# First halves of K of six tiles of head 0 computed between the opening modulation blocks, into idle PSUM banks

## What is computed

```python
def hybrid_layer(x, ctx, c, c_ctx, ...):
    mod_lat = jax.nn.silu(c) @ w_ada + b_ada
    mod_ctx = jax.nn.silu(c_ctx) @ w_ada + b_ada
    ...
    p = (rmsnorm(x, norm_w) * (1.0 + sc) + sh) @ w_in
    pc = (rmsnorm(ctx, norm_w) * (1.0 + sc_c) + sh_c) @ w_in
    ...
    x = x + gt * (jnp.concatenate([y_a, y_b], axis=-1) @ w_out)
```

## Time and profile before

| | |
|---|---|
| median of three runs | 2515.84 us (2508.7 to 2517.73) |
| profiled execution | 2515.01 us |
| its span in the profile | 2513.2 us |
| TensorE busy | 2322.5 us, 92% of the span |
| VectorE, ScalarE, GpSimd busy | 1392.0 (55%), 922.2 (37%), 147.3 us (6%) |
| DMA | 328.93 MB, 131 GB/s in the mean |
| mean granted TensorE clock | 0.973 |

### The profile page before, as it was taken

The page is one execution under the profiler, slowest core; times in us unless marked ns, Lnnn a source line. Parts: engine busy times, 40 slices in busy tenths (PEclk is TensorE's granted clock), DMA queues, the critical chain, the costliest instruction groups (busy, mean ns, idle before and its releaser), DMA issues. The chain is left out here.

```text
span 2513.2 us, 38542 instructions
## 1 busy us (share of the span) xinstructions
PE 2322.5 (92%) x13846; PEld 1893.7 (75%) x13846; DVE 1392.0 (55%) x2345; ACT 922.2 (37%) x1695; POOL 147.3 (6%) x187
## 2 busy tenths in 40 slices
PE   6799999999999999999999879999999999999797
PEld 3168787878778787878788658788787878878696
DVE  0334646555564646555654455657656575665654
ACT  3432424242423324242522364342424334242423
POOL 0000000000000000000100300000001000000002
PEclk8899999999999999999999979999999999999898
DMA  8973435242433434352535524343424333342453
GB/s 320 352 221 107 142 95 151 84 141 85 125 109 108 129 100 146 88 151 80 158 117 169 175 85 134 99 121 83 127 78 123 101 102 111 89 130 75 138 163 119
DMA packets 488018, 328.93 MB, mean 131 GB/s; under 512 B 48658, under 2 KB 452278, under 8 KB 487174
## 3 DMA queue, kind: packets, MB, share of 16 engines
q1 hardware_dynamic: 393174, 218.59, 31.0%
q10 hardware_dynamic: 94704, 109.13, 13.3%
q0 software_dynamic: 64, 0.20, 0.0%
HBM read 304.73 MB, written 23.13 MB: 130 GB/s over the span
## 5 line engine op out<-in xcount | busy, mean ns | idle before, releaser
L1712 PE MATMUL ps<-h_hi,w_hi 128*128 128x512 f32 (+1 forms) x2080 | 824.3, 396 | 19.1 <-DVE w_lo L1072 10.9
L1714 PE MATMUL ps<-h_hi,w_lo 128*128 128x512 f32 (+1 forms) x2080 | 765.9, 368 | 0.0
L1713 PE MATMUL ps<-h_lo,w_hi 128*128 128x512 f32 (+1 forms) x2080 | 764.2, 367 | 0.0
L1072 DVE TENSOR_TENSOR w_lo<-w_raw,w_hi 128x1024 fp32r<-128x1024 f32 (+1 forms) x332 | 399.5, 1204 | 319.0 <-ACT w_hi L616 269.8
L616 ACT CAST w_hi<-w_raw 128x1024 fp32r<-128x1024 f32 (+1 forms) x332 | 342.0, 1030 | 421.2 <-PE ps L1714 174.9
L1712 PEld LDWEIGHTS ps<-h_hi,w_hi 128*128 128x128 f32 x2080 | 399.1, 192 | 123.0 <-issue 52.4
L1714 PEld LDWEIGHTS ps<-h_hi,w_lo 128*128 128x128 f32 x2080 | 396.8, 191 | 67.6
L1713 PEld LDWEIGHTS ps<-h_lo,w_hi 128*128 128x128 f32 x2080 | 399.9, 192 | 47.7
L1072 DVE TENSOR_TENSOR arena<-arena,ps 128x512 f32<-128x512 f32 (+1 forms) x192 | 117.7, 641 | 109.2 <-PE ps L1803 107.8
L1974 PE MATMUL ps<-h_hi,w_hi 128*128 128x512 f32 (+1 forms) x448 | 160.0, 357 | 13.4 <-DVE h_lo L1072 13.1
L1572 POOL TENSOR_SCALAR small<-small 128x4 f32<-128x4 f32 (+3 forms) x51 | 20.6, 404 | 2300.3 <-DVE small L1425 1017.8
(11 more groups left out here) (191 smaller groups left out, 2692.4 us busy)
## 6 DMA issues: line engine op xcount, KB each, us to landing
w_raw<-in_w_in SPq DMA_DIRECT2D x260, 512.0 KB, 4.0
ada_raw<-in_w_ada ACTq DMA_DIRECT2D x128, 512.0 KB, 4.4
w_raw<-in_w_out SPq DMA_DIRECT2D x64, 448.0 KB, 3.8
arena<-in_w_ada SPq DMA_DIRECT2D x27, 512.0 KB, 8.3
w_raw<-in_w_ada SPq DMA_DIRECT2D x19, 512.0 KB, 8.4
ada_raw<-in_w_ada SPq DMA_DIRECT2D x18, 512.0 KB, 8.3
arena<-decay_rows ACTq DMA_DIRECT2D x16, 512.0 KB, 5.4
x_channel_major<-arena ACTq DMA_DIRECT2D x1, 4096.0 KB, 17.3
```

Source lines behind the costliest of these rows:

```text
L1072: return V.tensor_tensor(o, a, b, op)
L1712: mm(o, w_hi[:, s, k], h_hi[:, kt, t0:], start=kt == 0, stop=False)
L1713: before_last = mm(o, w_hi[:, s, k], h_lo[:, kt, t0:], start=False, stop=False)
L1714: last = mm(o, w_lo[:, s, k], h_hi[:, kt, t0:], start=False, stop=kt == KT - 1)
```

## The change

Six first halves (the small tile and tiles 0 to 4 of head 0; `FIRST[0:6]`) are loaded, split and multiplied in groups 4 to 7 of the opening, three pieces for every two blocks, each tile into a bank of its own (PJ, PJ + 1, G0 to G3). Their second halves follow in the old places. Units are numbered in the new order: 0 to 5 the first halves, 6 to 11 the second halves, then both halves of tiles 5, 6, 7. `w_raw` is out of the ring, which has five buffers now; eight loads of units stand between the blocks in SP's order (`W_AT`), the later ones behind a wait for `w_split`. The splits follow the modulation in each group (`EARLY_SPLITS`). In head 0 the multiplies of w_ada use banks A0 and A1, behind a wait for `rows_copied`.

```diff
-RING = RAW + 5
+EARLY = 6
+RING = 5
...
-        ada_ring = [w_raw[:, s] for s in range(RAW)] + [ada_raw[:, s] for s in range(2)] + [spare[:, s] for s in range(3)]
+        ada_ring = [ada_raw[:, s] for s in range(2)] + [spare[:, s] for s in range(3)]
...
+        FIRST = [(t, half) for half in range(2) for t in range(-1, EARLY - 1)] + [
+            (t, half) for t in range(EARLY - 1, TILES) for half in range(2)]
+        W_AT = {16: 0, 18: 1, 30: 2, 38: 3, 46: 4, 48: 5, 54: 6, 62: 7}
+        EARLY_SPLITS = {2: (0,), 3: (1,), 4: (2, 3), 5: (4,), 6: (5,), 7: (6, 7)}
+        FIRST_SPLITS = {5: 10, 13: 11, 21: 12, 29: 13, 37: 14}
...
 # SP, opening
             for u in range(2 * ADA_START):
...
+                if u in W_AT:
+                    first_unit(W_AT[u])
                 if u >= RING:
                     sp.wait_ge(ada_used, u - RING + 1)
...
 # w_unit
-                if isinstance(i, int) and i * UNITS + u < RAW:
-                    sp.wait_ge(ada_used, last_use[s] + 1)
-                else:
+                if not (isinstance(i, int) and i * UNITS + u < RAW):
                     sp.wait_ge(w_split, i * UNITS + (u - RAW + 1))
...
 # ACT (and DVE with split_lo)
-                if g == 7:
-                    split_hi(0, 0)
                 q = modulated_after(g)
                 if q >= 0:
                     modulate(0, range(4 * q, 4 * q + 4))
+                for u in EARLY_SPLITS.get(g, ()):
+                    split_hi(0, u)
...
 # PE
+            def early_piece(n):
+                u, k = n // HALF, n % HALF
+                if k == 0:
+                    pe.wait_ge(w_split, u + 1)
+                pe.wait_ge(h_ready, k + 1)
+                last = unit_piece(u, tile_bank(0, 0, FIRST[u][0]), 0, 0, [k])
+                if k == HALF - 1:
+                    last.then_inc(w_used, 1)
             for g in range(ADA_START // 4):
                 for pair in range(8):
                     u = 8 * g + pair
+                    for n in range(3 * (u - 32) // 2, 3 * (u - 31) // 2) if u >= 32 else ():
+                        early_piece(n)
                     pe.wait_ge(ada_loaded[u % RING], 16 * (u // RING + 1))
...
                     def ada(k):
...
+                        if is_first(layer, i):
+                            pe.wait_ge(rows_copied, 1)
...
+                            early = is_early(layer, i, t)
+                            u = EARLY + 1 + t if early else base + 2 + k
...
+                            if not (early and half == 0):
+                                last = unit_piece(u, tile_bank(layer, i, t), tokens(layer, t), half,
+                                                  [2 * (s % 4), 2 * (s % 4) + 1])
```

More of the change, by code:

```diff
@@ L507, in load_x, with w_unit, first_unit @@
                 sp.dma_start(x_in[:, n % 2], toks[n // 2][(n % 2) * P:(n % 2 + 1) * P, :]).then_inc(x_loaded[n % 2], 16)
+            def w_unit(i, u, source, tiles=HALF):
+                s = u % RAW
+                if not (isinstance(i, int) and i * UNITS + u < RAW):
+                    sp.wait_ge(w_split, i * UNITS + (u - RAW + 1))
+                    sp.sem_inc(sp_step, 1)
+                dst = w_raw[:, s, 0:tiles]
+                if source.shape[-1] == T:
+                    dst = dst.rearrange("p k n -> p (k n)").rearrange("p (k n) -> p k n", n=T)
+                sp.dma_start(dst, source).then_inc(w_loaded[s], 16)
+            def first_unit(u):
+                t, half = FIRST[u]
+                col = COLUMN[t] if t >= 0 else N_IN - P
+                w_unit(0, u, w_in[0].rearrange("(k p) n -> p k n", p=P)[:, half * HALF:(half + 1) * HALF, col:col + P])
             load_x(0)
@@ L540, in _ @@
                 w_cols = w_in[layer].rearrange("(k p) n -> p k n", p=P)
-                for half in range(2):
+                for half in range(2 if layer else 0):
                     w_unit(0, base + half, w_cols[:, half * HALF:(half + 1) * HALF, N_IN - P:N_IN])
@@ L591, in body @@
                         output_part()
+                        return
+                    if is_first(layer, i):
+                        for u in range(len(W_AT), 2 + UNITS):
+                            first_unit(u)
                         return
@@ L1167, in _ @@
                     modulate(0, range(4 * q, 4 * q + 4))
+                for u in EARLY_SPLITS.get(g, ()):
+                    split_lo(0, u)
             for layer in range(DEPTH):
@@ L1178, in _ @@
                 else:
-                    for u in range(1, LEAD + 1):
-                        split_lo(0, base + u)
+                    for u in range(len(W_AT), len(W_AT) + 2):
+                        split_lo(0, u)
                 vec.wait_ge(x_stored, 16 * (1 + layer * KT))
@@ L1647, in ada_multiply @@
                 for hf in range(2):
-                    pe.wait_ge(ada_loaded[RAW + hf], loads[hf])
+                    pe.wait_ge(ada_loaded[hf], loads[hf])
                     for j in range(HALF // 2):
@@ L1676, in rms, with unit_piece @@
                 spread_rms(n, c0, A1)
+            def unit_piece(u, bank_, t0, half, ks, both=False):
+                s = u % SPLIT
+                for k in ks:
+                    kt = half * HALF + k
+                    o = ps[:, bank_, t0:]
+                    mm(o, w_hi[:, s, k], h_hi[:, kt, t0:], start=kt == 0, stop=False)
+                    before_last = mm(o, w_hi[:, s, k], h_lo[:, kt, t0:], start=False, stop=False)
+                    last = mm(o, w_lo[:, s, k], h_hi[:, kt, t0:], start=False, stop=kt == KT - 1)
+                return (before_last, last) if both else last
+            def early_piece(n):
[6 more added lines that the diff above has]
+                    last.then_inc(w_used, 1)
             for g in range(ADA_START // 4):
@@ L1704, in _ @@
                     rms(layer, 0)
[L1706 to L1711, removed]
-                        mm(o, w_hi[:, s, k], h_hi[:, kt, t0:], start=kt == 0, stop=False)
-                        before_last = mm(o, w_hi[:, s, k], h_lo[:, kt, t0:], start=False, stop=False)
-                        last = mm(o, w_lo[:, s, k], h_hi[:, kt, t0:], start=False, stop=kt == KT - 1)
-                    return (before_last, last) if both else last
                 if layer == 1:
```

76 lines of the change are left out of this document (42 added, 34 removed).

## The result

The changed kernel takes 2551.12 us (median of four, 2547.27 to 2554.30), the kernel before 2516.78 beside it: a ratio of 1.0138, interval 1.0106 to 1.0170. A later set of runs gave 2553.29 against 2513.53, 1.0156 (1.0122 to 1.0190). It is slower by 34 to 40 us, 1.4 to 1.6%. The forecast was 2546 in a range of 2522 to 2558. One slow execution, the profiled one of the version with late splits (2666.45 us at a granted clock of 0.83), is left out of all numbers that follow.

What follows compares the result with a forecast made beforehand. TensorE was taken to bound the run, except the opening, paced by loads. Terms +5.4 + 10.0 + 37.9 - 22.4 = +30.9 us on the profiled 2515.0 gave 2546; own range 2531 to 2556, widened by rivals to 2522 to 2558.

Steps and rivals of the forecast that it cites:

- Term 1: Opening, ends of groups 0 and 1: five buffers and two early w_in loads cost +5.4 us, bounds 0 and 6.
- Term 2: Group 3: unit 2's load waits in SP's order for unit 0's split, holding block 30; +10.0 us, bounds 8 and 12.
- Term 3: Groups 4 to 7 become TensorE's, paying form changes and lost sharing; +37.9 us, bounds 17 and 44.
- Term 4: Behind the last turn to tile 4's end: 69.1 us against 91.5, so -22.4 us; bounds -30 and -14.
- (a): Opening: blocks in hand outlast SP's waits, switching is free, pieces fill the gaps; 2505 us, not slower; chance 5%.
- (b): Opening: the pace is right but SP isn't held, without the ring's 5.4 us too; 2525 us; chance 15%.
- (c): Head 0 gives back only 12 us, as table and multiplies wait for loads and clock stays low; 2556 us; 20%.
- the sum of 2543: Second stretch: by the Trainium skill sustained activity brings full clock back, at most some 3 us; sum 2543 us.
- the bounds of the terms: Limits per term: 0 and 6, 8 and 12, 17 and 44, -30 and -14 us; said to give 2531 to 2556.

Runs made afterwards that it cites:

- the version with late splits: Units 8 to 11 split in slots 4, 8, 12, 16 of head 0, against the version of the slots' edit; 2503.66 us, 0.9967 of the kernel before.
- the ring alone: The kernel before with one edit: the ring of blocks without w_raw's two buffers, five instead of seven; 2528.56 us, 1.0030 of the kernel before.
- the moved loads: The changed kernel with loads of units 0 to 3 and 6 at other places in SP's order; 2529.80 us, 1.0075 of the kernel before.
- the best versions: The slots' edit (2506.49 us), the version with late splits (2503.66), and that with six pieces ahead of every fourth block (2502.30, again 2505.78).
- the earlier splits: The changed kernel with all splits of the opening ahead of their group's modulation; 2537.20 us, 1.0069 of the kernel before.
- the slots' edit: Head 0's multiplies in slots 9, 14, 22, 30, added to the changed kernel with splits first, loads moved, three pieces per pair; 2506.49 us, 0.9960.

## Why the prediction was right, point by point

| term | predicted | measured |
|---|---|---|
| 1. ring and two early loads, to the turn of group 2 | +5.4 | +6.2 (+3.1 in the second profile) |
| 2. SP held ahead of block 30, group 3 | +10.0 | +11.1 |
| 3. groups 4 to 7 | +37.9 | +39.2 |
| 4. behind the last turn, to tile 4's end | -22.4 | -20.2 |
| sum | +30.9 | +36.3 |

*Term 1.* The size holds, with a spread of 3 us between two profiles of one kernel (the first is just above the bound of 6). Its halves are not shown: 2.7 us were put for the ring and 2.7 for the two early loads, but the ring alone lost 5.55, which leaves the loads less than the spread. That the smaller ring costs nothing from group 3 on was wrong by itself (the ring alone lost 0.8 and 1.3 us in groups 6 and 7); the changed kernel doesn't show it, as TensorE is the pace there.

*Term 2.* Block 30 was to land 16.5 us behind the turn (10.85 + 4.3 + 1.35); it was used 16.8 us behind it (68.11 to 84.90). With the 3.2 us for a load that the prediction took from the Trainium skill (DMA: Bandwidth & Descriptors, Anatomy of one DMA) the estimate would have been 15.4. The page gives that formula for DMAs that GpSimd issues, and these go out by SP; the rows of this case were the better source. What the term missed is the clock: after 10.47 us of idle the two last blocks and the turn ran at half clock. Moving the load gives group 3 back its old length, so the mechanism is shown.

*Term 3.* Groups 5 and 7 were summed at 19.5 and took 19.46. The two prices in it are each shown by a comparison of two versions: 0.33 us for a change of form and back (4.45 against 4.12), 0.85 for the lost sharing (4.12 against 3.27). For groups 4 and 6, 21.8 was summed; group 6 took 21.89, with a wait of 2.36 where 2.4 had been put. Group 4's 23.01 comes near it by another way, which is luck: there is no wait ahead of block 38, but half clock at the group's start. The prediction had let a wait of 2.4 us take in the half clock; the half clock was 3.5 us, and TensorE came to block 38 only 16.8 us behind the turn (90.77 to 107.56), when it had landed. The Trainium skill (TensorEngine Tiling (Array Packing), Key Properties) says that a change of tiling mode drains the engine. The trace agrees, with 0.33 us for a change and back.

*Term 4.* The sum of idle times was put at 24.9 us and measured at 21.5 (10.75, 0.67, 1.50, 0.92, 2.66 and 0.30, 0.28, 4.20 and 0.23); the second and third multiply waited less than summed. Yet the part was 2 us longer than predicted. The mis-sized term is the half clock: 4.4 us were put for it. At a granted clock of 0.78 in this part against 0.91 before, it comes to about 10 us, if what is missing to 71.3 us after idle time (21.5) and the work at full clock (33.0 + 4.9 + 1.8) is laid to it. The granted clock gives 9.2 us, summed over stretches of half a microsecond as busy time at the lower level, halved. So the total is partly luck, since the waits were put too long and the half clock too short. In the second profile of the changed kernel the waits are 24.3 us and the half clock 6.3 by the same sum, and the part is as long (75.31 to the rotation against 75.12): the two profiles share it out differently.

*The rivals.* (a) needed five blocks to outlast SP's wait; 10.47 us of idle say no. (b) is ruled out by the same row for this kernel, and the moved loads show about what it would have been: 2530 with the ring's cost still in it, where 2525 was given without. (c), a head 0 that gives back 12, is excluded by the 20.2. The Trainium skill (TensorE: Matmul & The Clock Gate, Part 1) says that sustained activity brings the full clock back. The trace agrees for groups 4 to 7 (0.96 against 0.92), but group 3 went to 0.68 and the part behind to 0.78, so the sum of 2543 by that page was further off than the forecast.

*The range.* The prediction says that 2531 to 2556 comes from the bounds of the terms. The bounds as given add up to 2510 and 2563 (-5 and +48 us), so the narrower range was a judgement and not a sum.

*Behind tile 4* the profiled runs differ by 2.8 us more (39.3 by the spans, 36.5 at the rotation), with the same order of instructions; this is within the spread of runs of one kernel and I give no cause.

## What to carry to other kernels

Many gaps of 0.3 us are not room for work in lumps of 0.7: here 1.04 us of pieces went in for each block, and each time a change of form was paid and the sharing of the array by neighbouring blocks was lost. Put such work between whole pairs; that gave back 1.18 us a pair. A load that waits for a late signal must not stand in a queue ahead of loads that something else needs; look for each wait that a queue gains, and count how long the buffers in hand last. When a stage gets half as long, everything that was timed by its slots (chains between engines, loads one step ahead) must be placed anew. Even so the best versions gained 8 to 11 us by the medians, for 33 us of work moved.

## What the runs showed that I had not expected

The ring's two buffers were worth about as much as the whole of the final gain: the kernel before with five buffers is 9 us slower by the medians, partly behind the opening, where its order is unchanged. A wait can move instead of going: of the 8.9 us that TensorE won behind the last turn by the earlier splits, 3.4 came back at the evacuation, as the loads that follow now ran beside a store of 4 MB, and 1.6 at the modulated tokens. And half clock must be added to the waits: in head 0 it took 9 to 10 us against 21.5 of idle, the slots' edit, which took away 5 us of waits, gave 8.8, and 2.4 and 2.5 us of waiting in group 6 cost 0 and 3 us more, by the level at which TensorE went on.
